# Moving the weight splits of the padding unit and the first output unit from ahead of level 0 to levels 2 and 3 of the triangular inverse

## What is computed

```
h = rmsnorm(x); proj = h @ w_in                    # q, k, v, gate z, b, a; attention q, k, v
group A, 4 heads of 128, chunks of 64: short conv + silu on q, k, v, then gated delta rule
    a = strict_lower((k*beta) @ k.T * decay);  lower = I + a
    u = lower^-1 @ (v*beta);  w = lower^-1 @ (k*beta*exp(gc))
    scan over the chunks with a 128x128 state per head, gated rmsnorm
group B, 8 query heads of 64, 2 kv heads: sliding window attention with sinks
x = x + concat(A, B) @ w_out
x = x + relu(rmsnorm(x) @ w1)^2 @ w2
```

## Time and profile before

| | us |
|---|---|
| median of 3 runs | 2776.21 |
| lowest and highest | 2772.47 and 2779.73 |
| the profiled execution, its own time | 2775.43 |
| its span, first to last instruction | 2773.9 |
| PE busy in the span | 2680.9 (97%) |
| DVE, ACT, POOL busy | 1467.4, 1015.7, 125.7 |
| mean granted PE clock | 0.988 |

### The profile page before, as it was taken

How to read it: one execution, slowest core, us unless ns; L and a number is a source line. 1 busy time by engine, 2 the same in 40 slices (tenths; PEclk the granted TensorE clock), 3 DMA queues, 4 the chain that set the end, 5 groups by cost and what they waited for, 6 DMA issues and landing times.

```text
span 2773.9 us, 38889 instructions
## 1 busy us (share of the span) xinstructions
PE 2680.9 (97%) x13726; PEld 2220.6 (80%) x13726; DVE 1467.4 (53%) x2205; ACT 1015.7 (37%) x1821; POOL 125.7 (5%) x157
## 2 busy tenths in 40 slices
PE   5999999999999999999999999999999999999998
PEld 4778878888878887888887887888888788788887
DVE  6566464364665536435465554634556555563454
ACT  4445332223454533222345453322234544322222
POOL 0011000000001100000000110000000011000000
PEclk9999999999999999999999999999999999999999
DMA  4210123234321012323332001223333200233242
GB/s 184 91 46 1 39 86 99 97 99 145 137 84 39 1 52 86 99 98 111 132 138 76 31 1 61 91 99 99 132 115 132 69 24 1 69 99 99 99 136 76
DMA packets 62027, 233.74 MB, mean 84 GB/s; under 512 B 7232, under 2 KB 7232, under 8 KB 61120
## 3 DMA queue, kind: packets, MB, share of 16 engines
q1 hardware_dynamic: 55728, 203.09, 22.2%
q0 software_dynamic: 6160, 28.84, 2.8%
HBM read 223.52 MB, written 8.39 MB: 84 GB/s over the span
## 4 chain that ended last, share of the span: by engine, by line
PE 79%; issue 17%; ACT 1%; POOL 1%; DVE 1%; POOLq 0%; DVEq 0%; ACTq 0%
PE ps L1092 77%; PE ps L1211 1%; PE ps L1300 1%; POOL pp L320 1%; ACT xi L575 0%; PE ps L1280 0%; POOL xi L330 0%; DVE h_l L1031 0%; DVE acc L676 0%; POOL qkvz L337 0%; DVE eg L998 0%; ACT ti L565 0%; DVE eg L1003 0%; ACT dt L592 0%; DVE h_l L1009 0%
## 5 line engine op out<-in xcount | busy, mean ns | idle before, releaser
L1092 PE MATMUL ps<-h_h,w_h 128*128 128x512 f32 x2016 | 798.4, 396 | 28.1 <-DVE h_l L1031 9.1
L1092 PE MATMUL ps<-h_h,w_l 128*128 128x512 f32 x2016 | 785.6, 390 | 0.0
L1092 PE MATMUL ps<-h_l,w_h 128*128 128x512 f32 x2016 | 785.4, 390 | 0.0
L668 DVE TENSOR_TENSOR w_l<-stage,w_h 128x1024 fp32r<-128x1024 f32 (+1 forms) x385 | 473.9, 1231 | 302.0 <-ACT w_h L367 288.6
L367 ACT CAST w_h<-stage 128x1024 fp32r<-128x1024 f32 (+1 forms) x385 | 399.0, 1037 | 552.8 <-PE ps L1092 543.8
L1092 PEld LDWEIGHTS ps<-h_h,w_h 128*128 128x128 f32 x2016 | 378.7, 188 | 129.1 <-DVE w_l L668 13.6
L1092 PEld LDWEIGHTS ps<-h_l,w_h 128*128 128x128 f32 x2016 | 379.0, 188 | 81.0 <-issue 4.8
L1092 PEld LDWEIGHTS ps<-h_h,w_l 128*128 128x128 f32 x2016 | 378.8, 188 | 79.7
L1092 PE MATMUL ps<-ff_h,w_h 128*128 128x512 f32 x1024 | 400.0, 391 | 0.0
L1092 PE MATMUL ps<-ff_h,w_l 128*128 128x512 f32 x1024 | 398.4, 389 | 0.0
L1092 PE MATMUL ps<-ff_l,w_h 128*128 128x512 f32 x1024 | 398.4, 389 | 0.0
(11 more groups left out here) (155 smaller groups left out, 2430.9 us busy)
## 6 DMA issues: line engine op xcount, KB each, us to landing
stage<-w SPq DMA_DIRECT2D x385, 512.0 KB, 3.3
x_next<-x POOLq DMA_DIRECT2D x20, 512.0 KB, 6.3
xs<-x POOLq DMA_DIRECT2D x4, 2048.0 KB, 8.5
out<-xs POOLq DMA_DIRECT2D x32, 256.0 KB, 2.3
bia<-bias POOLq DMA_DIRECT2D x1, 1536.0 KB, 7.2
cst<-con SPq DMA_DIRECT2D x1, 1152.0 KB, 5.6
prm<-par SPq DMA_DIRECT2D x1, 38.5 KB, 1.8
```

The lines of the kernel that those rows point to most:

```text
L668: dve.tensor_tensor(w_l[:, b, 0:k], stage[:, s, 0:k], w_h[:, b, 0:k].bitcast(F32), ALU.subtract).then_inc(w_lo.sem, 1)
L1092: return pe.matmul(o, a, b, start=start, stop=stop)
```

## The change

The two splits leave their place ahead of the first level, on ACT and on DVE. The padding unit is split after the attention step of level 2, the first output unit after the attention step of level 3, in the first pair only. On ACT these are the loop's passes `l == 3` and `l == 4`, since ACT's loop counts one higher. Sizes, buffers and semaphores stay as they are.

```diff
@@ scalar engine, pair q @@
                     attend("query")
-                    if q == 0:
-                        split_hi(g, CONV, U_PAD - CONV, 1)
-                        split_hi(g, CONV, U_OUT - CONV)
                     for l in range(1, LEVELS + 1):
                         for a in range(2):
                             n = q * 2 * LEVELS + 2 * (l - 1) + a
                             act.wait_ge(p_x.sem, p_x.after(g, n + 1))
                             act.copy(xi[:, a], heads(ring(a, 3 * l + 1))).then_inc(x_ready.sem, 1)
                         attend(f"level{l - 1}")
+                        if q == 0 and l == 3:
+                            split_hi(g, CONV, U_PAD - CONV, 1)
+                        if q == 0 and l == 4:
+                            split_hi(g, CONV, U_OUT - CONV)
@@ vector engine, pair q @@
                     attend("query")
-                    if q == 0:
-                        split_lo(g, CONV, U_PAD - CONV, 1)
-                        split_lo(g, CONV, U_OUT - CONV)
...
                         attend(f"level{l}")
+                        if q == 0 and l == 2:
+                            split_lo(g, CONV, U_PAD - CONV, 1)
+                        if q == 0 and l == 3:
+                            split_lo(g, CONV, U_OUT - CONV)
```

## The result

The changed kernel takes 2814.61 us (median of 4 runs, 2811.59 to 2817.54) against 2775.36 us before (4 runs): ratio 1.014, 95% interval 1.012 to 1.016. It is 39 us slower, where 17 were predicted. The direction was right, the size was not: 2814.6 lies above the range of 2782 to 2808, near the rival with one long slow stretch.

What follows compares the result with a forecast made beforehand. It took PE as the bound, with waits for `d` and slow clock behind them. Per group 13.67 us added less 9.33 removed gave +4.34, four groups +17.4, so 2793.6 us; own range 2785 to 2803, widened to 2782 to 2808.

Steps and rivals of the forecast that it cites:

- What bounds the kernel: PE, busy 97% of the span; in level 0, first pair, it waits 2.96 us for `d`, then runs slowly.
- What is removed: Levels 0 to 2, first pair: 27.57 us shrink to 18.24 without the splits, a gain of 9.33 us per group.
- The two waits: PE waits for `d` behind the moved splits: 2.88 us added at level 3, 4.65 at level 4, per group.
- The clock: Levels 3 and 4: clock falls at both waits, recovers as each level ends; 3.07 us each, 6.14 per group.
- rival (a): One slow stretch spans both waits: 2803 us through level 4, 2826 if also through level 5; chance 0.13.
- the attention step with outputs is dense enough: Behind the new waits, attention work denser than level 0's, which lacks outputs, supported slow stretches ending with the level.
- its own bounds for the two splits: Wait added at level 3 2.7 to 3.6 us, level 4 4.65 up to 5.6; +1 to +7 in four groups.
- (b): Only the longer wait, at level 4, drops the clock: +1.27 us per group, 2781 us; chance 0.08.
- (c): The clock stays high through both waits, levels 3 and 4: -1.8 us per group, 2769 us; chance 0.06.
- (d): The splits fall into DVE's free time, so the whole 9.33 us per group is gained: 2739 us; chance 0.05.

Runs made afterwards that it cites:

- e1_casts_early: The changed kernel with both ACT casts one pass earlier (l == 2 and l == 3), DVE's splits left where the change put them; 2741.82 us, ratio 0.988.
- e4_filled: The changed kernel with additional PE products in the two waits, 11 ahead of u in level 3 and 20 in level 4; 2773.11 us.
- e2_pad_waits: The changed kernel with both ACT casts in pass 3, so that only the split of level 3 makes PE wait; 2787.87 us.
- e3_out_waits: The changed kernel with ACT's casts in passes 2 and 4, so that only the split of level 4 makes PE wait; 2785.62 us.
- e7_dense_after: e3_out_waits with twelve additional products of 128 columns behind u of level 4, ahead of its attention step; 2783.71 us.
- e6_dve_later: The changed kernel with ACT's casts left in passes 3 and 4 and DVE's splits one level later; 2741.48 us, ratio 0.989.
- e8_old_place_casts_first: The kernel before, splits ahead of level 0, with ACT's two casts moved in front of its attention step query; 2763.43 us, ratio 0.996.
- e5_before_filled: The kernel before with four additional PE products of 256 columns in the wait of level 0, first pair; 2764.89 us, ratio 0.997.

## Why the prediction was wrong

**What bounds the kernel: right.** All that moved is time in which PE waits for `d` in the first pair, or runs at the low clock behind it.

**What is removed: right in mechanism, a tenth too large.** In the first group 9.18 us came off level 0 to 2 (9.33 predicted). Over the run, e1_casts_early gains 33.5 us where 4 x 9.33 = 37.3 were counted. The sum took the first group for all four. In the kernel before, the six levels took 47.45, 47.24, 47.05 and, in the last group, 2278.75 - 2231.81 = 46.94 us (the window in the earlier trace rows runs 0.51 us past their end). With 38.26 per group in e1_casts_early that makes 35.6. The rest lies outside the levels. One part of it can be seen at 39 us, in the input projection of the first group, in code that the change doesn't touch. PE waits 1.93 us for `w_l` there in both kernels; the clock then stays high in the profiled execution of the kernel before and falls in that of the changed kernel (in this order):

```profile
39.20:42.20 3.00, 3.00 (x14) 1.00 0.94 344
...
39.00:42.00 3.00, 3.00 (x8) 0.50 0.86 344
```

It falls there in e1_casts_early too. So the first y of level 0 comes at 184.11 and 183.80 in place of 182.76, and that of level 3 at 202.50, not at the 201.0 of the prediction. Another 1.5 us are PE's waits for POOL's `pp` in the second pair, 3.0 us in four groups of e1_casts_early against 1.5 in two before.

**The two waits: right.** 2.86 and 4.93 us seen, 7.67 per group in price, 7.53 predicted. The order of events was the predicted one: pass 3 of ACT ends with the small cast, and DVE's small split starts 4.75 us after DVE had come free. That small split takes 0.29 us (0.2 taken, 0.91 beside POOL), the large one 1.23 (1.22 taken). The rule of the Trainium skill (SBUF — State Buffer, section Who interferes with whom) is borne out: without POOL beside them both are short. In e1_casts_early the large split at 209.38 and POOL's product at 209.53 meet, and this time it is POOL that comes off worse, with 1.76 us in place of 0.83; nothing waits for it.

**The clock: this step failed.** The prediction said: "I take the slow stretch to end with the level, both times". That term was 6.14 us per group, 24.6 in all. It measured 41.5 us (the change against e4_filled). The long stretches last 34.0, 23.8, 34.0 and 20.3 us, and the fourth group has a short one of 3.3 besides. The restart is slow, and then the levels themselves, run at the low clock, do not reliably bring the high one back. The earlier trace rows had a stretch of 13.4 us, longer than the rest of a level; had I carried that length over to the new waits, rival (a) would have come out as the likeliest. The argument that the attention step with outputs is dense enough did not hold: the clock was back about where the level ended in the last group of e2_pad_waits, at the first wait of the fourth group of the changed kernel, and in the first group of e3_out_waits (at 222.4, with y of level 5 at 221.37), and in none of the others. One part of the term erred the other way: behind the first wait u was still fast or half fast (2.00 to 2.92 us), where 3.68 was taken. e7_dense_after supports the idea behind the argument: with more work behind u the clock came back before level 5 in all four groups of its profiled execution.

The medians add up. From e1_casts_early, with neither waits nor slow stretches: waits +31.3 (e4_filled), slow clock +41.5, together 2814.6. Less the 33.5 by which the kernel before stands above e1_casts_early, this is +39.3. The prediction had 30.1 + 24.6 - 37.3 = 17.4. Of the 21.9 missed, 16.9 are the clock's, 3.8 the gain's and 1.2 the waits'. A slip in the range changes little: by its own bounds for the two splits it should begin 1 us below the forecast, where it says 1 above.

**The rivals.** (a) is nearest: in three groups of the profiled execution one stretch runs over the second wait from before it, in two of them through level 5; its two figures, 2803 and 2826, enclose the result. (b) is out: the first wait brings the clock down as well, in the change and alone (e2_pad_waits). (c), waits with the clock staying high, is what e4_filled brought about by filling them: 2773, where 2769 was worked out. (d) is what e1_casts_early and e6_dve_later do, at 2742 instead of 2739; it wanted the cast and the split one level apart. The Trainium skill (TensorE: Matmul & The Clock Gate, section HAM oscillation) spoke against the change, and rightly, but the prediction leaned on it too far. The gaps that the section warns of are longer than the first wait, so it foretold only the second fall; the traces show the fall behind 2.86 us as well, and behind 1.74. And what a fall costs here differs from gap to gap, with stretches of 3 to 24 us behind a single wait.

What stays open: why the same wait is followed by a stretch of 3 us in one group and of 20 in another. More work behind the wait went with shorter ones (e7_dense_after); what decides group by group was not tried.

## What to carry to other kernels

When work on one engine needs a partner's output, look at where the partner stands in its own order, not at the level's name: here ACT's loop ran one level late, and a level's distance between cast and split was worth 73 us. A wait of PE can cost, beyond what it idles, a slow stretch whose length isn't fixed; with work like that of these levels behind it (small products with a weight load each), reckon with the longest stretch seen, not with one that ends where the code's level ends. A kernel whose runs scatter (2776 to 2803 us in e2_pad_waits, 2741 to 2743 in e1_casts_early) may be showing this; removing the wait narrows the spread as well.

## What the runs showed of the hardware that was not expected

- The low clock behind one wait lasted from 3.3 us (e2_pad_waits, 2.9 us of waiting) to 23.8 us (e8_old_place_casts_first, 1.74 us of waiting); e2_pad_waits has 3.3 and 20.3 us in one execution behind equal waits. The 34 us of the changed kernel hold a second wait.
- PE was busy without a gap for 20.3 us at the low clock (e2_pad_waits, 208.5 to 228.8), and the high one did not return in that time.
- A wait of 1.74 us, in e8_old_place_casts_first, was enough for the low clock in all four groups. With fillers that left 1.2 us of waiting (e5_before_filled), one group in four fell. A wait of 1.93 us in the input projection was followed by the low clock in the changed kernel and not in the kernel before.
- Twelve products per group added on the critical path (e7_dense_after) did not make the kernel slower than e3_out_waits, 2783.7 against 2785.6 us.
